# TensorE's wait for split weights in a hybrid encoder step: once for every unit, or once for two units

## The reference

```python
D_MODEL = 1024; D_FF = 4096; A_INNER = 2048; A_HEADS = 4; A_DH = 512
up = h @ w_up                                   # mLSTM, 1024 x 4096
q = jnp.einsum('bthd,hde->bthe', xc_h, w_q)     # and k, v: four heads of 512 x 512
return out @ w_down                             # 2048 x 1024
o.reshape(...) @ w_o                            # attention layers, 1024 x 1024
def _sq_relu_mlp(h, w1, w2):
    return jnp.square(jax.nn.relu(h @ w1)) @ w2
```

## The kernel before

| stage | layers | units in a group | groups |
|---|---|---|---|
| up | 0, 3 | 8 | 8 |
| qkv (mLSTM q, k, v; loop at L2491) | 0, 3 | 4 | 12 |
| down, bo, co (output projections, hh_stage, L1940) | 0 and 3, 1, 2 | 16, 8, 8 | 2 |
| bqkv | 1 | 8 | 6 |
| dq, dkv, uq, ukv | 2 | various | |
| ff1 (xg_stage, with xg_group, L1824) | all | 8 | 8 |
| ff2 (chunk, L2529) | all | 32 | 2 |

## Time and profile before

### The profile page before, as it was taken

One profiled execution on the slowest core, in us unless ns is written; L12 is line 12 of the kernel. 1 busy time (PEld: TensorE's weight loads), 2 busy tenths in 40 slices (PEclk: granted clock), 3 DMA queues, 4 the chain that ended last, 5 costly groups with the idle time before them and its releaser, 6 DMA issues.

```text
span 1797.3 us, 34006 instructions
## 1 busy us (share of the span) xinstructions
PE 1762.9 (98%) x13183; PEld 1641.1 (91%) x13183; DVE 1142.1 (64%) x1858; ACT 876.2 (49%) x1472; POOL 160.4 (9%) x111
## 2 busy tenths in 40 slices
PE   7999999999999999999999899999999999999998
PEld 6999855999999989999998699999999965999998
DVE  5886577575556546664575676554887567666544
ACT  4565422455444375554444555544665432455543
POOL 0000132110011001000120020010100034110000
PEclk9999999999999999999999999999999999999999
DMA  5565334555555624555544155555565424555553
GB/s 163 164 168 168 97 118 164 191 162 164 171 167 166 189 68 144 164 164 172 167 117 124 35 159 170 165 162 167 155 177 171 151 76 160 185 160 172 165 169 103
DMA packets 156171, 272.94 MB, mean 152 GB/s; under 512 B 22725, under 2 KB 28306, under 8 KB 156058
## 3 DMA queue, kind: packets, MB, share of 16 engines
q1 hardware_dynamic: 156058, 271.37, 48.6%
HBM read 250.55 MB, written 20.78 MB: 151 GB/s over the span
## 4 chain that ended last, share of the span: by engine, by line
PE 88%; DVE 8%; ACT 3%; DMA 1%; issue 1%; SPq 0%; DVEq 0%; ACTq 0%
PE PS L1796 86%; PE PS L1801 2%; ACT PB L960 1%; DVE C L1344 1%; DVE WLO L1067 1%; DVE QT L1379 0%; DVE NB L1335 0%; DMA out_p_C_dram<-CPST 0%; DMA RAWT<-in_c_w_ukv_dram 0%; DMA XIN<-in_x_sample_dram 0%; DVE TMP L1654 0%; DVE QT L1384 0%; DVE BST L1321 0%; DVE KS L1311 0%; DVE HL L1390 0%
## 5 line engine op out<-in xcount | busy, mean ns | idle before, releaser
L1067 DVE TENSOR_TENSOR WLO<-RAWT,WHI 128x512 fp32r<-128x512 f32 (+1 forms) x904 | 635.6, 720 | 481.7 <-ACT WHI L658 479.7
L658 ACT ACTIVATE WHI<-RAWT 128x512 fp32r<-128x512 f32 (+1 forms) x904 | 555.1, 626 | 648.2 <-PE PS L1796 645.6
L1796 PE MATMUL PS<-XGH,WHI 128*128 128x288 f32 x1776 | 526.7, 297 | 4.7 <-DVE WLO L1067 4.0
L1796 PE MATMUL PS<-HH,WHI 128*128 128x288 f32 (+1 forms) x1792 | 528.8, 295 | 0.4 <-issue 0.4
L1796 PE MATMUL PS<-HH,WLO 128*128 128x288 f32 (+1 forms) x1792 | 527.5, 294 | 0.0
L1796 PE MATMUL PS<-HL,WHI 128*128 128x288 f32 (+1 forms) x1792 | 527.1, 294 | 0.0
L1796 PE MATMUL PS<-XGH,WLO 128*128 128x288 f32 x1776 | 523.7, 295 | 0.0
L1796 PE MATMUL PS<-XGL,WHI 128*128 128x288 f32 x1776 | 523.4, 295 | 0.0
L1796 PEld LDWEIGHTS PS<-XGH,WHI 128*128 128x128 f32 x1776 | 333.9, 188 | 8.3 <-DVE WLO L1067 4.8
L1796 PEld LDWEIGHTS PS<-HH,WHI 128*128 128x128 f32 x1792 | 336.5, 188 | 3.9 <-issue 3.6
L1796 PEld LDWEIGHTS PS<-HH,WLO 128*128 128x128 f32 x1792 | 336.6, 188 | 0.0
(11 more groups left out here) (364 smaller groups left out, 1420.1 us busy)
## 6 DMA issues: line engine op xcount, KB each, us to landing
RAWT<-in_w_ff_dram SPq DMA_DIRECT2D x256, 512.0 KB, 3.7
RAWT<-in_a_w_up_dram SPq DMA_DIRECT2D x64, 512.0 KB, 3.7
RAWT<-in_a_w_down_dram SPq DMA_DIRECT2D x32, 512.0 KB, 3.6
RAWT<-in_b_w_qkv_dram SPq DMA_DIRECT2D x24, 512.0 KB, 3.8
RAWT<-in_a_w_q_dram SPq DMA_DIRECT2D x16, 512.0 KB, 3.7
RAWT<-in_a_w_k_dram SPq DMA_DIRECT2D x16, 512.0 KB, 3.6
RAWT<-in_a_w_v_dram SPq DMA_DIRECT2D x16, 512.0 KB, 3.7
C<-in_state_mlstm_C_dram SPq DMA_DIRECT2D x8, 1024.0 KB, 5.9
```

Of the source, the lines that this page charges most:

```text
L658: act.activation(hi, raw, ACT.Copy).then_inc(weight_hi, 1)
L1067: dve.tensor_tensor(lo, raw, hi, ALU.subtract).then_inc(weight_lo, 1)
L1796: return pe.matmul(out, lhsT, rhs, start=start, stop=stop, **kw)
```

## The change

unit gets a parameter, units: with 1 it waits for weight_lo of its own unit as before, with 2 for its own and the next, and with 0 it doesn't wait. Callers pass 2 at even and 0 at odd units of a group in: ff1 from its third group on; the second group of the output projections; all q, k, v groups but the first; and ff2, except the first eight units of its first group. The last four units of the program (last_units) and the stages up, bqkv, dq, dkv, uq and ukv stay as they were.

```diff
--- before.py
+++ after.py
@@ -1803,9 +1803,10 @@
             def kblock(t, k):
                 return t[:, bass.ds(k, 1), :].rearrange("p a t -> p (a t)") if not isinstance(k, int) else t[:, k, :]
 
-            def unit(u, slot, b, cols, rh, rl, start, stop, var=None):
-
-                pe.wait_ge(weight_lo, u + 1)
+            def unit(u, slot, b, cols, rh, rl, start, stop, var=None, units=1):
+
+                if units:
+                    pe.wait_ge(weight_lo, u + units)
                 for a, (c, m) in enumerate(cols):
                     if a == 2 and var is not None:
                         pe.wait_ge(var_out, var + 1)
@@ -1821,14 +1822,14 @@
 
                 pe.wait_ge(group_out, g + (st.g0 - 1))
 
-            def xg_group(st, g, b, nu=None, cols=FOUR, var=None, after={}):
+            def xg_group(st, g, b, nu=None, cols=FOUR, var=None, after={}, pairs=False):
 
                 banks_free(st, g)
                 for k in range(DB):
                     if nu is not None and k % 4 == 0:
                         pe.wait_ge(xg_lo, 2 * nu + k // 4 + 1)
                     unit(8 * g + (st.u0 + k), k % SPL, b, cols, XGH[:, k, :], XGL[:, k, :], k == 0, k == DB - 1,
-                         var if k == 0 else None)
+                         var if k == 0 else None, 2 * (1 - k % 2) if pairs else 1)
                     if k in after:
                         after[k]()
 
@@ -1934,8 +1935,8 @@
                     stat(nu, st.g0)
                     xg_group(st, 1, 1, var=nu)
                 with pe.Fori(1, st.groups // 2) as q:
-                    xg_group(st, 2 * q, 0)
-                    xg_group(st, 2 * q + 1, 1)
+                    xg_group(st, 2 * q, 0, pairs=st.name == "ff1")
+                    xg_group(st, 2 * q + 1, 1, pairs=st.name == "ff1")
 
             def hh_stage(st, ready):
 
@@ -1945,7 +1946,7 @@
                         if g == 0:
                             ready(k)
                         unit(st.u0 + st.upg * g + k, k % SPL, g, FOUR, HH[:, k, :], HL[:, k, :],
-                             k == 0, k == st.upg - 1)
+                             k == 0, k == st.upg - 1, units=2 * (1 - k % 2) if g else 1)
 
 
             pe.wait_ge(const_in, 32)
@@ -2496,7 +2497,8 @@
                         banks_free(st, x)
                         for k in range(4):
                             f = 4 * h + k + (16 if m == 2 else 0)
-                            unit(st.u0 + 4 * x + k, k, x % 2, FOUR, HH[:, f, :], HL[:, f, :], k == 0, k == 3)
+                            unit(st.u0 + 4 * x + k, k, x % 2, FOUR, HH[:, f, :], HL[:, f, :], k == 0, k == 3,
+                                 units=2 * (1 - k % 2) if x else 1)
                     last_state = mlstm_mix(i, la)
 
                     def ready(k):
@@ -2532,7 +2534,8 @@
                         for k in range(n):
                             kk = 8 * j + k
                             unit(8 * j + (st.u0 + 32 * g + k), k % SPL, g, FOUR, kblock(HH, kk), kblock(HL, kk),
-                                 start and k == 0, stop and k == 7)
+                                 start and k == 0, stop and k == 7,
+                                 units=1 if start and g == 0 else 2 * (1 - k % 2))
 
                     chunk(0, True, False)
                     with pe.Fori(1, 3) as j:
```

## The result

The changed kernel is slower, but by less than was forecast. Its median is 1802.67 us (twelve runs, 1801.17 to 1806.32), that of the kernel before 1799.11 us (twelve runs, 1796.61 to 1802.95): a ratio of 1.0022, 95% interval 1.0013 to 1.0031, or +3.6 us. The forecast was 1808.0 us. Of the 5.3 us between it and 1802.67, 2.4 are the base (the three runs shown ahead of the prediction had a median of 1801.53, the twelve of 1799.11) and 2.9 the effect (6.5 forecast, 3.6 found). In two further comparisons the changed kernel gave 1.0026 [1.0015, 1.0037] and 1.0025 [1.0016, 1.0035], so about 4.4 us by the mean of the three ratios (1.0024). The profiled execution took 1805.26 us, its span is 1803.1 us.

What follows compares the result with a forecast made beforehand. TensorE, busy 98% of the span, was taken to set the pace. New waits of 7.2 us less 0.7 for removed ones gave +6.5 us: 1801.53 + 6.5 = 1808.0 us, range 1803.8 to 1812.0.

Steps and rivals of the forecast that it cites:

- Is the delay given back?: TensorE's long waits behind the late places end on ACT or DVE work fed by TensorE, so nothing comes back.
- the removed waits: 274 waits dropped, some 105 pairs in the slower pace at 0 to 13 ns each: 0.7 us given back.
- the redrawing of the pace: Matmul stream's two paces drawn anew: no term in the sum, 1.5 us either way in the forecast's own range.
- 4.2 + 0.17 + 2.9 us: New waits: seven residual stages at 0.60 us each, last layer's ff2 0.17, second q, k, v groups 2.9.
- the later wait swallows the earlier one: In second groups DVE's later splits don't hang on TensorE's late unit, so delays don't add: 0.60 us a residual stage.
- ff1 covered: In ff1, lo(5) is done 0.27 us before unit 4 starts, against 0.05 needed: cost 0.
- rival "paid back": Later TensorE waits behind q, k, v and residual stages shrink by the delay: 1800.8 us with all of it, chance 0.04.
- None ends on a DMA: TensorE's long waits behind the late places all end on ACT or DVE work, so the delay moves them too.
- slower pace disappears: Fewer waits end the slower matmul pace in some 350 units, 4.5 us back: 1804.2 us, chance 0.08.
- The load of unit 6 stands 0.05 us behind lo(7): Trace sign in second groups: unit 6's opening weight load follows lo(7) by 0.05 us, instead of lo(6).
- 19 waits more, 7 us in sum: Trace sign: TensorE waits for WLO at L1067 about 19 times more, about 7 us in sum.
- three signs of being wrong: DVE's lo(4) and lo(5) row moves with TensorE, later TensorE waits shrink, or 748 matmuls turn to 741 in long stretches.

Runs made afterwards that it cites:

- Experiment 7: Changed kernel with DVE's four norm operations of the second group behind the split of unit 7 instead of unit 5; one run, 1801.44 us.
- experiment 8: Changed kernel with POOL's squares of half 0 held back behind unit 8 (output projections and ff2); 1803.0 us against 1799.28 before, ratio 1.0021.
- Experiment 2: Changed kernel with single waits again in the ten late places, 254 of 274 waits still removed; 1796.36 us against 1797.44 before, ratio 0.9994.
- experiment 1: Changed kernel cut to waits in pairs in ff1 alone, every other stage waiting as before; 1796.70 us against 1797.44 before, ratio 0.9992.
- Experiment 14: Kernel before with weight_lo's wait repeated inside each unit, 2675 more waits, all satisfied; 1799.11 us against 1798.23, ratio 1.0003.
- 15: Kernel before with waits in pairs only in ff1 of layers 0 and 1; one run, 1796.55 us.
- 6: Changed kernel cut to waits in pairs in the q, k, v stage alone; one run, 1800.00 us.
- 9: The changed kernel unedited, timed a third time, on one chip with the kernel that keeps both waits; 1802.28 us against 1797.57 before, ratio 1.0025.
- 10: Changed kernel with the odd unit's own wait kept too, so none is removed; 1803.52 us against 1797.57 before, ratio 1.0030.

## Why the prediction was right and wrong

The places, the cause and the size of the loss were right. What failed is the step "Is the delay given back?", which put everything beyond the sum at nothing because no long wait of TensorE ends on a DMA. One does: TensorE's wait for QR, with a tile of w_ukv two engines behind it. The prediction held the DMAs fixed ("no DMA ... changes"), but that tile landed up to 1.9 us earlier in the changed kernel, and 1.4 us came back there, though not as the delay paid back. Two more terms of the sum were off: the removed waits, put at 0.7 us, gave none, and the redrawing of the pace, put at nothing with 1.5 us either way, came to 1.8 us by the profiles, which may be chance. And the base, 1801.53 us from three runs, was 2.4 us too high.

**The places and sizes of the new waits: right.** All of 4.2 + 0.17 + 2.9 us is in the table of steps. In the residual stages the size came from one thought, that DVE's queue at lo(6) and lo(7) depends on nothing TensorE does late, so that the later wait swallows the earlier one; the second step is 0.22 to 0.29 us and not 0.60, as that demands. Experiment 7 shows what makes the second step and 8 what makes the first. Experiment 2 shows that outside these places there is no loss to measure.

**ff1 covered: right.** No step in any profile, and experiment 1 is not slower. The margin of 0.27 us held.

**The removed waits, 0.7 us: wrong, they give 0.** The middle between 0 and 13 ns was taken, because the wide interval stood behind a wait. Experiment 14 puts a satisfied wait at 0.3 ns, at most 0.9, and experiment 1 shows the same stage time with and without 24 of them in either pace. The wide interval belongs to the pace and not to the wait. The rule of the Trainium skill cited in the prediction (TensorE: Matmul & The Clock Gate, section Step-by-step: what each phase is for), that the load is pulled ahead under matmuls in flight, speaks for 0, and the runs agree with it. This term was off in the other direction, so the miss of the rest is 0.7 us larger. (A slip beside it: the rival "paid back" was said to decide once more than 3.6 us come back; with 6.5 us forecast and 3.6 as the limit it is 2.9.)

**"None ends on a DMA": wrong, 1.3 to 1.5 us.** The list names the last engine, DVE with QR; ACT ahead of it stood at a DMA for 2.5 us. The chain had to be followed one engine further. What the rival described, that the delay is paid back, is still not what happened: the time comes back where there is no delay (1, 15) and doesn't where there is one (6). It comes with pairs in a looped stage of the first two layers. These make TensorE's instruction stream shorter (33846 instructions in the changed kernel, 34006 before; all of the 160 are operations on registers on TensorE, and the kernel that keeps both waits has 33846 too, so it isn't the waits themselves), and the second tile of w_ukv then lands in 3.7 to 4.0 us instead of 5.1 to 5.7. The transfer of instructions ahead of uq also moves, by 3 to 4 us, as a shorter stream lets one expect, but it is over some 30 us before that tile is issued. What makes the tile land earlier stays open.

**The pace, taken as zero with 1.5 us either way: by the profiles 1.8 us in favour.** The changed kernel had 199, 257, 270 slow units (without ff1 241) and the one before 376, 394, 394: 137 fewer by the medians of the three, and at 13 ns each 1.8 us. It was seen only with the removed waits and all the stalls together: with both waits kept there are 424 and 438, with removed waits and no stalls 415 and 671, and with half of the stalls gone or moved 431 and 390. This is a part of the rival "slower pace disappears", and its reason, that the waits keep the pace up, is contradicted by 1 and 2. What chooses the pace stays open. The profiles are few, the other kernels spread from 343 to 730, the timed runs of 9 and 10 don't show the difference that the counts ask for, and chance isn't excluded. So these 1.8 us are not shown to belong to the change.

**The sum again.** 7.2 - 1.4 - 1.8 = 4.0 us for the changed kernel, where the three comparisons gave 3.6, 3.4 and 4.7 by their medians and 4.4 by the mean ratio; for both waits 7.2 - 1.4 + 0.5 (37 slow units more, by the medians) = 6.3, measured 6.7 and 5.9 by the medians, 6.1 and 5.4 by the ratios. The comparisons carry an uncertainty of about 2 us each, and the pace comes from few profiles, so the close agreement is partly luck; without the pace the sum is 5.8 for both kernels, which lies outside the interval of the first comparison (2.3 to 5.6) and inside those of the others (to 6.7 and 6.3 for the changed kernel). The range of the prediction began at 1803.8, and the measured median lies 1.1 us below it. It took both misses: the right base with the forecast effect gives 1799.11 + 6.5 = 1805.6, the base of three runs with the measured effect 1801.53 + 3.6 = 1805.1. The three runs shown agreed within 2 us with each other and turned out the three slowest of twelve.

**What the trace was to show.** The load of unit 6 stands 0.05 us behind lo(7): right. No new wait in ff1: right. "19 waits more, 7 us in sum": wrong in the list of waits of the matmuls by the way that it counts, nearly right in that of the weight loads (17 and 6.4), right in the starts of the units. Of the three signs of being wrong two came: a later wait shrank (QR, 1.9 to 0.3 us), and the count of 748 turned to 741 in the window at 752 us, while the one at 410 us turned the other way. DVE's row of lo(4) and lo(5) didn't move with TensorE.

## What to carry to other kernels

A wait that asks for more than the next step needs costs what the producer is behind at that place, and only the places where the producer has other work between two of its steps matter; removing waits that are already satisfied gave nothing here, so asking for two at once has no gain to set against it. Read the cost from when the producer's operation ends, per place, and add up late starts only where the producer itself depends on them. Follow each long wait of the bounding engine back over every engine to its first cause before you call it internal, and take the base from as many runs as the effect is small.

## What the runs showed of the hardware

- A satisfied semaphore wait ahead of a weight load costs TensorE 0.3 ns, at most 0.9 ns and perhaps nothing (2675 extra waits, ratio 1.0003 [0.9993, 1.0013]).
- From the end of DVE's split to the start of the weight load that waits for it TensorE takes 0.05 us (17 of the 19 new stalls of the changed kernel); at unit 0 of q, k, v, where a wait for the banks stands ahead of it, 0.12.
- The same stream of 128x288 matmuls has two paces, 1.577 and 1.590 us for twelve, and keeps one for tens of us. In the 18 profiles every one of more than 300 changes of pace came within three units behind a stall, in other places from one execution of a program to the next. Between 199 and 730 of the some 800 units that keep a pace were slow.
- A tensor_tensor on POOL slows DVE's beside it. Timeline of the changed kernel, lo(5) and POOL's second operation:

```profile
511.59 1.92 DVE L1067 TENSOR_TENSOR WLO<-RAWT,WHI 128x512 fp32r<-128x512 f32 x1
...
511.20 1.76 POOL L1721 TENSOR_TENSOR SQ<-SQ 128x576 f32<-128x576 f32 x1
```

  The split takes 1.92 us beside it and 0.68 alone; in experiment 8 four splits took 5.91 us beside POOL's, where four take 2.48 alone.
- A transfer's time can change by 1.9 us (5.7 to 3.8 us for one 512 KB tile, issued at the same place) between two programs that differ in TensorE's instructions alone. What does it stayed open.
